# The order of attention's instructions, found by forward and backward passes over a table of operations

## The reference

```python
h = modulate(rmsnorm(x, g_attn), shift1, scale1)       # adaLN, shift and scale from c @ w_ada
aq, ak, av, bq, bk, bv = split_cols(h @ w_in)          # one projection, two head groups
# group A: 8 query heads, 2 key/value heads of 64, rms-normalised q and k, rotary
p = softmax(s * HEAD_DIM ** -0.5); a_out = p @ v
# group B: 4 heads, two 64-wide softmax maps each, values of 128
a = p[:, :, 0] - lam * p[:, :, 1]; b_out = rmsnorm(a @ v, g_sub) * (1 - lam_init)
x = x + gate1 * (concat(a_out, b_out) @ w_o)
h = modulate(rmsnorm(x, g_ffn), shift2, scale2)
u = conv3(h @ w_up) + conv_b; g, v = split(u)
x = x + gate2 * ((silu(g) * v) @ w_down)
```

## Time and profile before

| | |
|---|---|
| median of 3 runs | 1715.58 us (1715.5 to 1716.35) |
| span of the profiled execution, its own time | 1715.9 us |
| instructions | 25956 |
| TensorE busy | 1643.9 us (96%) |
| VectorE busy | 1101.3 us (64%) |
| ScalarE busy | 773.7 us (45%) |
| GpSimd busy | 634.2 us (37%) |
| mean granted TensorE clock | 0.990 |

### The profile page before, as it was taken

The page is one execution under the profiler, slowest core; times in us unless marked ns, Lnnn a source line. Parts: engine busy times, 40 slices in busy tenths (PEclk is TensorE's granted clock), DMA queues, the critical chain, the costliest instruction groups (busy, mean ns, idle before and its releaser), DMA issues.

```text
span 1715.9 us, 25956 instructions
## 1 busy us (share of the span) xinstructions
PE 1643.9 (96%) x9530; PEld 1393.6 (81%) x9530; DVE 1101.3 (64%) x1728; ACT 773.7 (45%) x1281; POOL 634.2 (37%) x328
## 2 busy tenths in 40 slices
PE   5899999989999999999999999999989999999998
PEld 3778887768898888888888877788767888888887
DVE  7887678878965575676245774777665763353256
ACT  6546666553443312332133344676564543343343
POOL 0356562220132243333332307664322244444442
PEclk9899999999999999999999999999999999999999
DMA  9430000024223243444434422101112133223332
GB/s 394 176 109 26 26 26 26 26 98 185 80 97 106 98 135 100 133 125 132 136 111 134 147 98 87 38 14 38 38 34 103 62 112 99 97 98 98 95 93 95
DMA packets 44509, 168.24 MB, mean 98 GB/s; under 512 B 4736, under 2 KB 4736, under 8 KB 42496
## 3 DMA queue, kind: packets, MB, share of 16 engines
q1 hardware_dynamic: 41760, 158.08, 27.7%
q10 hardware_dynamic: 2656, 8.91, 1.4%
HBM read 161.73 MB, written 5.24 MB: 97 GB/s over the span
## 4 chain that ended last, share of the span: by engine, by line
PE 70%; DVE 6%; issue 3%; ACT 2%; POOL 1%; DMA 1%; DVEq 0%; ACTq 0%; POOLq 0%
PE ps L1289 21%; PE ps L1290 21%; PE ps L1291 21%; PE ps L1420 3%; PE ps L1434 2%; DVE sqsum L2261 1%; PE ps L1453 1%; POOL w_lo L1164 1%; DVE ht L2288 1%; PE ps L1454 1%; DVE junk_mid L2191 1%; DMA w_raw<-w_d 1%; DVE h_lo L2296 1%; ACT p_sb L1966 0%; ACT w_hi L1737 0%
## 5 line engine op out<-in xcount | busy, mean ns | idle before, releaser
L1164 POOL TENSOR_TENSOR w_lo<-w_raw,w_hi 128x1024 fp32r<-128x1024 f32 x175 | 441.3, 2524 | 915.4 <-ACT w_hi L1737 882.7
L1289 PE MATMUL ps<-h_hi,w_hi 128*128 128x512 f32 (+1 forms) x1592 | 567.7, 357 | 10.8 <-DVE h_lo L2296 6.5
L1290 PE MATMUL ps<-h_lo,w_hi 128*128 128x512 f32 (+1 forms) x1592 | 556.1, 349 | 0.0
L1291 PE MATMUL ps<-h_hi,w_lo 128*128 128x512 f32 (+1 forms) x1592 | 555.4, 349 | 0.0
L1289 PEld LDWEIGHTS ps<-h_hi,w_hi 128*128 128x128 f32 x1592 | 302.5, 190 | 59.3 <-issue 21.0
L1291 PEld LDWEIGHTS ps<-h_hi,w_lo 128*128 128x128 f32 x1592 | 302.3, 190 | 39.7
L1290 PEld LDWEIGHTS ps<-h_lo,w_hi 128*128 128x128 f32 x1592 | 302.9, 190 | 35.3
L1737 ACT ACTIVATE w_hi<-w_raw 128x1024 fp32r<-128x1024 f32 x188 | 198.4, 1056 | 227.9 <-PE ps L1291 209.8
L1289 PE MATMUL ps<-a_hi,w_hi 128*128 128x512 f32 (+1 forms) x552 | 191.6, 347 | 1.2 <-DVE a_lo L2678 1.2
L1290 PE MATMUL ps<-a_lo,w_hi 128*128 128x512 f32 (+1 forms) x552 | 191.3, 347 | 0.0
L1291 PE MATMUL ps<-a_hi,w_lo 128*128 128x512 f32 (+1 forms) x552 | 191.0, 346 | 0.0
(11 more groups left out here) (189 smaller groups left out, 2410.7 us busy)
## 6 DMA issues: line engine op xcount, KB each, us to landing
w_raw<-w_d SPq DMA_DIRECT2D x188, 512.0 KB, 3.5
ada_b<-ada_d SPq DMA_DIRECT2D x56, 512.0 KB, 4.3
ada_first<-first_d SPq DMA_DIRECT2D x8, 1024.0 KB, 20.3
ada_lead<-ada_d SPq DMA_DIRECT2D x14, 512.0 KB, 3.9
ada_mid<-ada_d SPq DMA_DIRECT2D x10, 512.0 KB, 7.8
x_sb<-x_d SPq DMA_DIRECT2D x2, 1536.0 KB, 8.8
x_sb<-x_d ACTq DMA_DIRECT2D x1, 3072.0 KB, 11.6
x_spill_d<-x_sb ACTq DMA_DIRECT2D x1, 2048.0 KB, 7.5
```

Of the source, the lines that this page charges most:

```text
L1164: nc.gpsimd.tensor_tensor(w_lo[:, c % RING, :], w_raw[:, c % RAW, :], w_hi[:, c % RING, :].bitcast(f32), ALU.subtract).then_inc(w_lo_done, 1)
L1289: nc.tensor.matmul(out, lh, rh, start=first, stop=False)
L1290: nc.tensor.matmul(out, lh, rl_, start=False, stop=False)
L1291: return nc.tensor.matmul(out, ll, rh, start=False, stop=last)
```

## The change

The table gets more operations and other durations, and the loop at its end is replaced.

- Loads of weight units and of the first modulation tiles become operations (LD) on SP or "first" (done at time 0), with a `lag` until they land. They stand in the table only: SP's code emits the same loads in the same order, and the loop over kind LU becomes a loop over unit numbers.
- WH needs its load and the WH before it, WL the WL before it, a QS the QS before it. The `ada` operations are made beside the units' weights and need their loads.
- S takes 1.46 and 0.76 us in the table, with a lag of -0.16, in place of 1.25 and 0.46. PE after PE needs no drain and no signal.
- `Turns.serve` is the same kind of simulation, forward along the needs or backward along the users. `in_turn` sorts by `pos` first, then in turn backward and forward, using each pass's end times as the next one's positions. It then tries 200 perturbed positions, each with two such rounds, and keeps the order with the smallest cost.

```diff
+LOAD_ISSUE, LOAD_LAG, MID_LAG = .5, 3.4, 9.
...
+            t, e = best[0], ENGINES[best[1]]
+            x = min((i for i in ready[e] if ready_at[i] <= t + .02), key=lambda i: (pos[i], i))
+            begin[x], end[x] = t, t + self.after[x]
+            now[e] = t + self.us[x] - OVERLAP[e]
...
+def in_turn(ops, trials=TRIALS):
+
+    turns = Turns(ops)
+    rng = np.random.default_rng(0)
+
+    def settle(pos, passes):
+
+        best = None
+        for _ in range(passes):
+            now, begin, end, order = turns.forward(pos)
+            cost = max(now["PE"], now["ACT"] - 2., now["DVE"] + 2., now["POOL"] - 6.)
+            if best is None or cost < best[0]:
+                best = cost, pos, begin, order
+            _, _, end, _ = turns.backward([-t for t in end])
+            pos = [-t for t in end]
+        return best
+
+    best = here = settle([x["pos"] for x in ops], 5)
+    for _ in range(trials):
+        start = np.array(here[1 + rng.integers(2)])
+        moved = rng.random(len(ops)) < rng.choice([.02, .1, .5, 1.])
+        found = settle(list(start + moved * rng.normal(0, rng.choice([.3, 1., 3.]), len(ops))), 2)
+        if found[0] <= here[0]:
+            here = found
+        if found[0] < best[0]:
+            best = found
...
+    def loaded(c):
+
+        before = split_units.get(c - RAW)
+        need, lag = [before and before["WL"]] + loads[-1:], LOAD_LAG
+        if l == 0 and c == wo_unit(l) + RING + RAW:
+            need, lag = need + [units[-1]["P"][-1]], MID_LAG
+        early = c < unit0(l) + RING + RAW
+        loads.append(op("first" if early else "SP", "LD", LOAD_ISSUE, 0, need, c=c, lag=lag))
+        return loads[-1]
+
+    def halves(c, pos, *need, load=None):
+
+        older = split_units.get(c - 1, {})
+        wh = op("ACT", "WH", 1.06, pos, [load or loaded(c), older.get("WH"), *need], c=c)
+        wl = op("POOL", "WL", 2.4, pos, [wh, older.get("WL")], c=c, WH=wh)
+        split_units[c] = dict(WH=wh, WL=wl)
+        return split_units[c]
...
-            s = op("PE", "S", 1.25 if wide else .46, at, need, it=it, qt=qt, qi=qi, pair=n_pair, before=prev_pair, front=front)
+            s = op("PE", "S", 1.46 if wide else .76, at, need, lag=-.16, it=it, qt=qt, qi=qi, pair=n_pair, before=prev_pair, front=front)
...
-                x = min((r[1] for r in ready if r[0] <= t + .02), key=lambda x: x["pos"])
...
+    order, now = in_turn(ops)
...
-            for x in plans[0]["order"]["SP"]:
-                load_unit(x["c"])
             next_unit = wo_unit(0) + RING + RAW + (KT - FIRST_OUT[0]) // 2
+            for c in range(wo_unit(0) + RING + RAW, next_unit):
+                load_unit(c)
```

More of the change, by code:

```diff
@@ L2 @@
 from contextlib import ExitStack
+import numpy as np
 import concourse.bass as bass
@@ L158, in unit_banks, with __init__, forward, backward @@
     return {0: (0, 1), 1: (2, 3), 2: (4, 5), 3: (6, 7), 4: (0, 1), 5: (2, 3), 6: (0, 1)}.get(u, (7, 7))
+ENGINES = ["PE", "ACT", "DVE", "POOL", "SP"]
+TRIALS = 200
+class Turns:
+    def __init__(self, ops):
+        at = {id(x): i for i, x in enumerate(ops)}
+        self.eng = [x["eng"] for x in ops]
+        self.us = [x["us"] for x in ops]
+        self.after = [x["us"] + DRAIN[x["eng"]] + x["lag"] for x in ops]
+        self.needs = [sorted({at[id(n)] for n in x["need"]}) for x in ops]
+        self.users = [[] for _ in ops]
+        for i, needs in enumerate(self.needs):
+            for j in needs:
+                self.users[j].append(i)
+    def forward(self, pos):
+        return self.serve(pos, self.needs, self.users)
+    def backward(self, pos):
+        return self.serve(pos, self.users, self.needs)
+    def serve(self, pos, needs, users):
+        open_needs = [len(n) for n in needs]
+        ready_at, begin, end = ([0.] * len(pos) for _ in range(3))
+        now = dict.fromkeys(ENGINES, 0.)
+        ready = {e: [] for e in ENGINES}
+        order = {e: [] for e in ENGINES}
+        freed = [i for i, n in enumerate(open_needs) if not n]
+        while True:
+            while freed:
+                i = freed.pop()
+                e = self.eng[i]
+                if e in ready and end[i] == 0.:
+                    ready[e].append(i)
+                    continue
+                for j in users[i]:
+                    f = self.eng[j]
+                    t = begin[i] + self.us[i] if e == f == "PE" else end[i] + SIGNAL[f]
+                    ready_at[j] = max(ready_at[j], t)
+                    open_needs[j] -= 1
+                    if not open_needs[j]:
+                        freed.append(j)
+            best = min(((max(now[e], min(ready_at[i] for i in r)), k) for k, (e, r) in enumerate(ready.items()) if r),
+                       default=None)
+            if best is None:
+                return now, begin, end, order
+            t, e = best[0], ENGINES[best[1]]
+            x = min((i for i in ready[e] if ready_at[i] <= t + .02), key=lambda i: (pos[i], i))
+            begin[x], end[x] = t, t + self.after[x]
+            now[e] = t + self.us[x] - OVERLAP[e]
+            ready[e].remove(x)
+            order[e].append(x)
+            freed.append(x)
@@ new lines, in in_turn @@
+def in_turn(ops, trials=TRIALS):
[20 more added lines that the diff above has]
+            best = found
+    order = {e: [ops[i] for i in turn] for e, turn in best[3].items()}
+    return order, best[0]
@@ L167, in op @@
         x = dict(kw, eng=eng, kind=kind, us=us, pos=pos, need=[n for n in need if n is not None], l=l)
+        x.setdefault("lag", 0.)
         ops.append(x)
@@ L276, in split @@
         y["LO"] = op("DVE", "LO", .95 if wide else .68, pos + .05, [y["HI"]], y=y)
-    out_wl = []
+    out_wl, split_units, loads, lead_loads = [], {}, [], []
+    def loaded(c):
[12 more added lines that the diff above has]
+        return split_units[c]
     def weights(c):
@@ L282, in weights @@
         y = units[u]
-        x = dict(c=c)
-        x["WH"] = op("ACT", "WH", 1.06, y["at"][-1] - .5, [y["P"][-1]], c=c, P=y["P"][-1])
-        x["WL"] = op("POOL", "WL", 2.4, y["at"][-1] - .5, [x["WH"]], c=c, WH=x["WH"])
+        if l == 0 and u < len(LEADS_AHEAD):
+            for n in range(sum(LEADS_AHEAD[:u]), sum(LEADS_AHEAD[:u + 1])):
+                need = [ada_ops[n - 4]] if n >= 4 else []
+                loads.append(op("SP" if need else "first", "LD", LOAD_ISSUE, 0, loads[-1:] + need, lag=LOAD_LAG, c=None))
+                lead_loads.append(loads[-1])
+                ada_op(n)
+        x = halves(c, y["at"][-1] - .5, y["P"][-1])
         if u + RING < IN_TILES:
@@ L289, in weights, with ada_op @@
             out_wl.append(x["WL"])
+    ada_ops = []
+    def ada_op(n):
+        c = FIRST_ADA + n
+        if c == 3 * KT:
+            plan["gate"] = op("DVE", "gate", .5, -20 + KT * .5, ada_ops[-1:])
+        ada_ops.append(op("DVE", "ada", 2.6, -20 + n * .5, ada_ops[-1:] + lead_loads[-1:], c=c))
     normed = []
@@ L303, in mixing_plan @@
         y["ST"]["need"] += [units[1]["EV"][-1]] if l == 0 else [units[2]["SQ"][-1], units[2]["EV"][-1]]
[L304 to L310, removed]
+    ada = ada_ops
     plan["ada"] = ada
@@ L560, in mixing_plan @@
                 op("DVE", "MID", 1.22, 900 + 2 * n + s, need, c=MID_ADA + n, s=s)
+    qs = []
     for b in range(B_HEADS):
-        op("ACT", "QS", .85 if l < DEPTH - 1 else .62, at_b[3] + .3 + .05 * b,
-           [it["done"] for it in heads[b] + heads[max(b, B_HEADS - 2)]], b=b)
+        qs.append(op("ACT", "QS", .85 if l < DEPTH - 1 else .62, at_b[3] + .3 + .05 * b,
+                     qs[-1:] + [it["done"] for it in heads[b] + heads[max(b, B_HEADS - 2)]], b=b))
     op("ACT", "TB", 1.5, 499, [t["LOT"]["need"][0] for it in heads[-1] for t in it["T"]])
@@ L590, in mixing_plan @@
         if d % 2:
[L591 to L595, removed]
+            halves(wo_unit(l) + RING + u, 700 + d, x["last"])
     for d in range(1, FIRST_OUT[l], 2):
@@ L628, in mixing_plan @@
         counts["PG"] = p["no"] = counts.get("PG", 0) + 1
-    for e in engines:
+    for e in ENGINES:
         for x in order[e]:
```

1 line of the change is left out of this document (removed).

## The result

The changed kernel takes 1694.36 us (median of 4 runs, 1693.27 to 1698.42) against 1715.96 before in the same session. The ratio is 0.9871, 95% interval 0.9854 to 0.9888, so 21.6 us or 1.3% faster. The forecast was 1705, half of the gain. The profiled execution of the changed kernel was the slowest of its four runs and spans 1696.6 us, 19.2 less than that of before; what follows compares these two.

The account below looks back on a forecast made before the run. TensorE's work plus its 72 us of idle time was taken as the bound. Savings of 12.65 us (idle time and clock) less 1.65 for a new VectorE stretch gave 11.0 off 1715.9: forecast 1705 us, range 1694 to 1720.

Parts of the forecast that it names:

- the named stretches: Four badly filled attention stretches (200-345, 345-398, 1070-1120, 1220-1304 us), where TensorE idles 29.0 us, the pool for savings.
- step 2: Better positions in attention save 3.0 us (200-345), 4.0 (345-398), 1.0 (1070-1120) and 3.0 (1220-1304) of TensorE's idle time.
- the two stretches that I held up as well filled: Attention at 125-200 and 1120-1220 us, where TensorE idles only 0.3 of 75 and 0.1 of 100 us.
- Clock: Three half-clock spells in attention (119, 355, 1085 us) cost 5.0 us; one of them goes, saving 1.65 us.
- step 3: The table's new score and load costs: SP has slack and the planner sees its wait, so 0 us.
- step 4: VectorE instructions stretched beside GpSimd, such as `oa_lo`: one new hit of 2.2 us, of which 1.65 reach TensorE.
- the slower rival: VectorE's stretches meet the tighter order in attention: 1722 us; chance of slower by over 0.2%: 0.16.
- step 5: Hand-over behind layer 0's attention: 0 lost of 7 to 8 us saved; 3 to 4 if VectorE's end stays.
- the one at 1694 us: Nearly all idle goes: 80% of the 29.0 us in attention, less 1.65, so -21.5 us; chance 0.17 (below 1699).

Follow-up runs that it names:

- passes_only: The changed kernel with the five forward and backward passes but without the 200 perturbed trials: 1707.60 us, ratio 0.9941.
- load_fix: The changed kernel, with each load in the planner's table beginning behind the issue of the one before, not its landing: 1685.09 us, ratio 0.9811.
- search_old_table: The changed kernel's whole search run on the old costs (scores 1.25 and 0.46 us, all loads at time 0): 1685.18 us, ratio 0.9813.

## Why the prediction was wrong in size

The direction and the mechanism held: the gain is idle time in the named stretches, and feed-forward takes 562 us as before. **What failed is step 2, the share of each stretch's idle time that a better order takes.** I took 11.0 of 29.0 us (4.0, 3.0, 3.0 and 1.0); measured are 6.5, 7.8, 7.0 and 2.4, together 23.7. Two reasons stood behind the small shares. The new order would make small errors of its own: it made few, 200 to 345 us idles 0.6% of its length, near the 0.4% and 0.1% of the two stretches that I held up as well filled. And 3.7 us of waits for `ptmp` at layer 0's end were put down to the softmax chain, of which filler would hide only some: from 104 to 386 us 0.7 us of them are left, with the same needs, so they too were order. I also did not separate the passes from the trials; passes_only saved 10.1 us, near my 11.0, and the trials brought the rest.

- *Clock:* 1.65 us were forecast. The spells at 355 and 1085 us are gone, and one of 3.3 us at 68 us that was left out of the count. A longer one came at 116 us and a new one at the hand-over (396 to 400 us), and the mean granted clock of the profiled execution is no better (0.989 for 0.990). It is a matter of the run too: two of the changed kernel's four runs had 0.992 and 0.993 and took 1693.3 us, the profiled one 1698.42. TensorE's busy time fell by 4.0 us all the same; this gain was not forecast, and its cause stays open.
- *The table's costs (step 3):* wrong. Loads were priced at 0 and the reason given, that the planner now sees SP's wait, hid that it sees loads one by one. The prediction's table of stretches also began at 125 us, so the place of the loss was in none of its rows. It cost 5.5 us of idle time from 60 to 125 us and most of a half-clock spell; mended, 10 us (load_fix).
- *VectorE's stretches (step 4):* TensorE waited once for `oa_lo`, 2.0 us for the 2.1 of before, where 1.65 were charged as new. The count on TensorE didn't change, so the charge was too much by about its size; the slower rival fell. Another stretch came outside attention, the tile of 3.17 us at the hand-over.
- *The hand-over (step 5):* the row was read rightly and 3 to 4 us were named as the loss if VectorE's end did not move, but 0 was taken, for 7 to 8 us saved in attention; 12.0 came. VectorE's list did end earlier (its last `pt_lo` at 384.6 us for 390.4), and 6.2 us were lost all the same, because the 5 us of tiles behind the list had stood in VectorE's wait for the squares and now stand in the open. The step's own rule gives this: VectorE's 4.1 us of slack and the 5.8 by which its list ended earlier are 9.9, less 2.0 for the long tile 7.9, and the reciprocal moved by 8.1.
- *The rivals:* the one at 1694 us, with 80% of the idle time gone, is what came, at 0.17. Its share was right (82%), and its sum only because two things it left out, the loads and the hand-over, were about made up by TensorE's shorter busy time and the small gaps elsewhere. That it hit the time is luck.

In the profiled pair the sum closes: 23.7 us from the four stretches, less 5.5 (ramp), 0.9 (125 to 200) and 4.2 (hand-over), and 2.2 from the stretches left over, are 15.3 us of idle time (72.0 to 56.7), and 4.0 of busy time make 19.3 for 19.2 measured.

What stays open: why load_fix also shortens the stretch from first scores to first squares (258 us for 261), and how much of the 12 us of the trials comes from which stretch.

## What to carry to other kernels

Where several in-order queues feed a nearly full engine and the order comes from hand-written priorities, a search can take most of the idle time that stands beside ready filler (82% here, where a third was forecast); and price separately what the next stage can take over, by the slack of the engine that it needs first. Check a planner's table against the trace for dependencies, not only durations: here one needless wait of a load for the landing of the one before cost 10 us, while the corrected durations gained nothing that shows (load_fix 32.4 us, search_old_table 32.1). Search a table with more than one seed before two tables are compared by a few us. Work that was placed in an engine's wait becomes visible when the wait goes; moving one tile of it into the stage that got room cut the loss from 3.2 to 0.8 us here.

## What the hardware showed that was not expected

A dot product of two SBUF tiles on VectorE (`junk_mid`, 128 x 1024), which takes 1.21 to 1.23 us in every one of its 20 instances before, took 3.17 us in the changed kernel when a GpSimd `w_lo` of 3.18 us ran beside it.

```profile
L2191 DVE CUSTOM_DVE_ANT_0 junk_mid<-ada_mid,c_mid x20: 1209/1224/1228, 384.8 to 450.2; 128x1024 bf16<-128x1024 f32 x20
```

```profile
L2286 DVE CUSTOM_DVE_ANT_0 junk_mid<-ada_mid,c_mid x20: 1211/1224/3172, 376.2 to 442.8; 128x1024 bf16<-128x1024 f32 x20
```

The `w_lo` began while the dot product before was running (387.05, against its end at 387.98) and took 3.18 us for the 2.40 of the one shown below, and the next dot product ended 1.1 us behind it, as if the two had taken turns. The dot products `junk_lead` of the same size read one operand from PSUM (`ps`). All 28 of them took 1.20 to 1.22 us, though GpSimd was busy 36 of the 65 us in which they stand:

```profile
L2268 DVE CUSTOM_DVE_ANT_0 junk_lead<-ada_lead,ps x28: 1200/1220/1222, 60.6 to 118.1; 128x1024 bf16<-128x1024 f32 x28
```

In load_fix two tiny adds on VectorE (128 x 8, L2310) took 3.36 us where the same two take 0.37 in the changed kernel. The engines' timelines, VectorE's and GpSimd's, show that GpSimd was in back-to-back work beside them in load_fix, and the second add ends at 96.09 us, just behind the `w_lo` that ends at 96.07. In the changed kernel GpSimd was idle from 86.4 to 92.0, around the adds at 88.16.

```profile
92.73 3.36 DVE L2310 TENSOR_TENSOR mod<-mod,sm 128x8 f32<-128x8 f32 x2
...
92.42 1.29 POOL L1292 TENSOR_TENSOR a_raw<-straight,swapped 128x512 f32<-128x512 f32 x1
93.67 2.40 POOL L1259 TENSOR_TENSOR w_lo<-w_raw,w_hi 128x1024 fp32r<-128x1024 f32 x1
```

So instructions of VectorE with two operands in SBUF, of 128 x 8 as of 128 x 1024, ended up to about a whole GpSimd instruction late here. That GpSimd is the cause is read from the times that coincide: no run takes the GpSimd instruction away, and what sets which instruction is hit was not looked into.
